# Prompt attention: small and large query blocks in turn

## The chip, the cores and the metric

The kernel runs on one core of one Trainium2 chip. The metric is the device time of one execution in microseconds (us), and for several runs their median. The core has five engines that work beside each other, each through its own list of instructions in program order: PE (matrix products and transposes), DVE (vector work), ACT (activations, copies), POOL and SP (here mostly issuers of DMAs). They wait for each other by semaphores.

## The reference

One decoder layer for a prompt of 16 meta tokens and 1024 tokens, and for 8 sequences of 4 new tokens over a paged cache. In order: norm and input projection, a retention group and an attention group (latent attention, 4 heads), output projection, a gated convolutional feed-forward, a last norm. The change concerns the attention of the prompt alone:

```
def block(args):                      # one block of 128 queries, starting at s0
    ql, qp, s0 = args
    qpos = s0 + jnp.arange(ATTN_BLOCK)
    return mla_attend(ql, qp, ((c_kv, k_pe, kpos[None, :] <= qpos[:, None]),))
...
s = (einsum('bqhc,bkc->bhqk', qf, c_kv) + einsum('bqhr,bkr->bhqk', pf, k_pe)) * SOFTMAX_SCALE
p = softmax(where(mask, s, -inf))     # over the keys
out = einsum('bhqk,bkc->bqhc', p, c_kv)
```

The mask is causal: query block j sees the keys of blocks 0 to j. Block 0 is the 16 meta tokens, blocks 1 to 8 hold 128 queries each. So block 0 has 16 keys, block 1 has 144, and block 8 has 1040.

## The kernel before

The program is a row of stages, each a block in which all five engines run their own lists and at whose end they meet: input projection, latents and retention, prompt attention, decode attention, output projection, feed-forward. Prompt attention works on 36 items (j, h), one for each query block j and head h, in the order of the list `items`: all heads of block 0, then of block 1, up to block 8. Item number i uses half i % 2 of the score banks, of the probabilities `pr` and of the turned probabilities `pt`; the bank of the output is a single one.

For one item:

- PE makes the scores, `score_part` (three products for each piece of up to 512 keys, L1228 to L1230). It waits until the exponentials of item i-2 have left the half (`exped`).
- DVE adds the causal mask on the last 128 columns (L1179), takes the row maximum (L1182) and turns it into the bias (L1190). This is `max_part`. For block 8 the meta keys have scores of their own in `meta_s`, with a maximum (L1182), a joining step (L1188) and later a sum (L1198) more.
- ACT takes the exponential and its row sum (L1145), `exp_part`.
- DVE inverts the sum (L1200) and scales the row (L1203), `scale_part`.
- PE turns the scaled rows, block by block of keys (L1261), `turn_part`, in groups of four blocks. Groups are numbered through all items; group n goes to turn bank n % 2 and waits until group n-2 was copied out. ACT copies the even groups (L1132), DVE the odd ones (L1134), `copy_turn`. An item of block 0 to 3 has one group, of block 4 to 7 two, of block 8 three (four blocks, four, one).
- PE multiplies with the values (L1272), `value_part`, when all groups are copied and the output bank is free (`lo_out` of item i-1).
- ACT takes the output out as a high part (L1152), DVE takes the low part by subtraction (L1208).

What sets the order is the loop of each engine, written out by hand:

```
PE:   score_part(i + 1);  value_part(i - 1);  turn_part(i)
DVE:  scale_part(i);  max_part(i + 1);  odd copies of item i;  lo_part(i - 1)
ACT:  exp_part(i + 1);  even copies of item i;  hi_part(i - 1)
```

SP and POOL meanwhile load six pages of the cache for the stage behind. They wait only for the page table.

Of the kernel before, what the change touches and what calls it, by code (L numbers as in the profile page):

```python
# [37 lines left out]
NT = 1 + SEQ // P  # L38
H, DK = 4, 128
# [16 lines left out]
def col0(j):  # L56
    return 0 if j == 0 else T0 + P * (j - 1)
# [991 lines left out]
def prompt_attention(kit, t, ident, kn, vt, qn, qp, kp, mh, ml, qn_s, qp_s, pages):  # L1049

    nc = kit.nc
    items = [(j, h) for j in range(NT) for h in range(H)]
    with ExitStack() as c:
        causal = kit.sb(c, "pa_causal", [P, P])
        meta_s = kit.sb(c, "pa_meta", [P, H, META])
# [8 lines left out]
        S = {n: kit.sem("pa_" + n) for n in (  # L1064
            "causal", "zero", "meta", "meta_out", "scored", "masked", "max_a", "max_b", "max_c", "exped", "sum_a", "sum_b", "scaled",
            "turned", "act_out", "dve_out", "out_done", "hi_out", "lo_out")}

        def geometry(i):

            j, h = items[i]  # L1070
            return (NS, META, 1) if j == 0 else (col0(j), P, j + 1)

        turns = []
        for i in range(len(items)):
            nb = geometry(i)[2]
            turns += [(i, b, min(b + 4, nb)) for b in range(0, nb, 4)]
# [7 lines left out]
        def scores(i):  # L1084


            j, nq = items[i][0], geometry(i)[1]
            two = score_b[0:nq, 2 * (i % 2):2 * (i % 2) + 2, :].rearrange("p b n -> p (b n)")
            if j < NT - 1:
                return [(two[:, 0:META + P * j], NS, META + P * j)]  # L1090
            return [(two[:, 0:P * j], T0, P * j), (meta_s[0:nq, items[i][1], :], NS, META)]

        with nc.Block() as block:
            @block.sync
            def _(sp):
                sp.dma_start(causal[:], t["causal"]).then_inc(S["causal"], 16)
                pages.load_table(sp)
                sp.wait_ge(pages.table, 16)
                for page in range(EARLY):
                    pages.load_sync(sp, 0, page)  # L1100
                for u in range(EARLY // UP2):
                    pages.wait_unit(sp, 0, u)
# [12 lines left out]
            def copy_turn(n, eng):  # L1115
                i, b0, b1 = turns[n]
                nq = geometry(i)[1]
                eng.wait_ge(S["turned"], n + 1)
                if i >= 2:
                    eng.wait_ge(S["out_done"], i - 1)  # L1120
                runs = []
                if b0 == 0:
                    runs.append((0, 1, T0))
                    b0 = 1
                if b1 > b0:
                    runs.append((b0, b1, P))
                for x0, x1, nk in runs:
                    off = (x0 % 4) * P
                    src = turn_b[0:nk, n % 2, off:off + (x1 - x0) * P].rearrange("p (b q) -> p b q", q=P)[:, :, 0:nq]
                    dst = pt[0:nk, i % 2, x0:x1, 0:nq]  # L1130
                    if n % 2 == 0:
                        m = nc.scalar.activation(dst, src, ACT.Copy)  # L1132
                    else:
                        m = nc.vector.tensor_copy(dst, src)  # L1134
                m.then_inc(S["act_out"] if n % 2 == 0 else S["dve_out"], 1)
# [29 lines left out]
            @block.vector  # L1165
            def _(dve):
                dve.wait_ge(S["causal"], 16)
                dve.wait_ge(S["meta"], H)
                dve.tensor_copy(meta_s[:], extra_b[:, 0, 0:H * META].rearrange("p (h m) -> p h m", h=H)
                                ).then_inc(S["meta_out"], 1)  # L1170
                dve.wait_ge(S["meta_out"], 1)

                def max_part(i):
                    j, nq = items[i][0], geometry(i)[1]
                    dve.wait_ge(S["scored"], i + 1)
                    parts = scores(i)
                    w = META if j == 0 else P
                    own = parts[0][0][:, parts[0][2] - w:]
                    dve.tensor_tensor(own, own, causal[0:nq, 0:w], ALU.add).then_inc(S["masked"], 1)  # L1179
                    dve.wait_ge(S["masked"], i + 1)  # L1180
                    for n, (region, _, _) in enumerate(parts):
                        m = dve.reduce_max(mx[0:nq, i, n:n + 1], region, AX_X)  # L1182
                    m.then_inc(S["max_a"], 1)
                    dve.wait_ge(S["max_a"], i + 1)
                    most = mx[0:nq, i, 0:1]
                    if len(parts) == 2:
                        most = mx[0:nq, i, 2:3]
                        dve.tensor_tensor(most, mx[0:nq, i, 0:1], mx[0:nq, i, 1:2], ALU.max).then_inc(S["max_b"], 1)  # L1188
                        dve.wait_ge(S["max_b"], i + 1 - H * (NT - 1))
                    dve.tensor_scalar(mx[0:nq, i, 3:4], most, -SCALE, None, ALU.mult).then_inc(S["max_c"], 1)  # L1190

                def scale_part(i):
                    j, nq = items[i][0], geometry(i)[1]
                    dve.wait_ge(S["exped"], i + 1)
                    total = sm[0:nq, i, 0:1]
                    if j == NT - 1:
                        total = sm[0:nq, i, 2:3]
                        dve.tensor_tensor(total, sm[0:nq, i, 0:1], sm[0:nq, i, 1:2], ALU.add).then_inc(S["sum_a"], 1)  # L1198
                        dve.wait_ge(S["sum_a"], i + 1 - H * (NT - 1))
                    dve.reciprocal(sm[0:nq, i, 3:4], total).then_inc(S["sum_b"], 1)  # L1200
                    dve.wait_ge(S["sum_b"], i + 1)
                    p = pr[0:nq, i % 2, NS:T0 + P * j]
                    dve.tensor_scalar(p, p, sm[0:nq, i, 3:4], None, ALU.mult).then_inc(S["scaled"], 1)  # L1203

                def lo_part(i):
                    h, (q0, nq, _) = items[i][1], geometry(i)
                    dve.wait_ge(S["hi_out"], i + 1)
                    dve.tensor_tensor(ml[:, H + h, q0:q0 + nq], out_b[:, 0, 0:nq],  # L1208
                                      mh[:, H + h, q0:q0 + nq].bitcast(F32), ALU.subtract).then_inc(S["lo_out"], 1)
                max_part(0)  # L1210
                for i in range(len(items)):
                    scale_part(i)
                    if i + 1 < len(items):
                        max_part(i + 1)
                    for n in range(first_turn[i], last_turn[i] + 1):
                        if n % 2:
                            copy_turn(n, dve)
                    if i:
                        lo_part(i - 1)
                lo_part(len(items) - 1)  # L1220
# [1714 lines left out]
def layer(nc, x, t, y):  # L2935
# [14 lines left out]
    with ExitStack() as c:  # L2950
# [17 lines left out]
        with ExitStack() as c1:  # L2968
            with ExitStack() as c2:
# [32 lines left out]
                with kit.phase():  # L3002
                    prompt_attention(kit, t, ident, kn, vt, qn, qp, kp, mh, ml, qn_s, qp_s, pages)
# [90 lines left out]
```

## Time and profile before

| | us |
|---|---|
| median of 3 runs (1625.48 to 1630.23) | 1627.07 |
| the profiled execution | 1625.34 |
| its span | 1623.7 |
| prompt attention in it, first work of the stage to the last subtraction | 462.30 to 604.30 |
| PE, DVE, ACT busy in the span | 1486.8, 817.5, 590.7 |

The span is what the trace covers; 1.6 us of the execution lie around it. All times below are us from the start of the span. "PEld" is the loading of weights on PE, which overlaps its products. The granted clock is PE's, as a share of 2.4 GHz; its lower level is 1.2 GHz, 0.50.

### The profile page before, as it was taken

The page shows a single profiled execution, that of the slowest core. Times are in us where ns is not written, and L with a number is a line of the kernel's source. Part 1 is how long each engine was busy: PE and PEld are TensorE (multiplying, and loading weights), DVE is VectorE, ACT ScalarE, POOL GpSimd, SP SyncE. Part 2 cuts the span into 40 slices and gives each one's busy share as a digit, 9 for nine tenths or more (in the row PEclk, how much of TensorE's full clock was granted, in tenths as well). Part 3 has the DMA queues.
Part 4 walks back from the last instruction along what each step waited for, and adds up shares of the span by engine and source line. Part 5 has one row for each costly group of instructions (what it writes and reads, how often), then busy time and mean ns, then how long its engine had stood idle before and what let it go on. Part 6 is the DMA issues. An engine that isn't in the chain of part 4 may idle for free. (4 is left out here: it accounts for less than half of the span.)

```text
span 1623.7 us, 26233 instructions
## 1 busy us (share of the span) xinstructions
PE 1486.8 (92%) x9453; PEld 1271.8 (78%) x9453; DVE 817.5 (50%) x1470; ACT 590.7 (36%) x1267; POOL 422.6 (26%) x543
## 2 busy tenths in 40 slices
PE   5999999897989989877997689999999999999997
PEld 5998888665867866555886679999999999778786
DVE  4422200153446644331156756666666565678877
ACT  5420111122433333222033354444544444534454
POOL 3236620130030005524003444443344342000000
PEclk9999999997979999888998899999999999999999
DMA  6422123514230005535132122333332333864764
GB/s 228 145 95 85 61 100 108 177 60 124 84 106 1 1 8 165 156 100 144 58 118 78 48 75 87 104 103 103 103 90 83 98 103 124 302 188 155 247 216 165
DMA packets 142989, 186.76 MB, mean 115 GB/s; under 512 B 22835, under 2 KB 89252, under 8 KB 142710
## 3 DMA queue, kind: packets, MB, share of 16 engines
q1 hardware_dynamic: 137038, 174.37, 33.2%
q0 software_dynamic: 4800, 9.84, 2.1%
q10 hardware_dynamic: 1056, 1.31, 0.3%
q8 instruction: 56, 0.92, 0.2%
q14 instruction: 39, 0.32, 0.1%
HBM read 149.25 MB, written 36.19 MB: 114 GB/s over the span
## 5 line engine op out<-in xcount | busy, mean ns | idle before, releaser
L2779 PE MATMUL p_ff<-s_xh,s_ff_rhi 128*128 128x266 f32 x608 | 178.9, 294 | 33.7 <-ACT s_ff_u L2354 16.8
L2779 PE MATMUL p_ff<-s_ff_th,s_ff_rhi 128*128 128x266 f32 x640 | 183.9, 287 | 0.4 <-DVE s_ff_u L2586 0.4
L2782 PE MATMUL p_ff<-s_ff_th,s_ff_rlo 128*128 128x266 f32 x640 | 183.4, 287 | 0.0
L2781 PE MATMUL p_ff<-s_ff_tl,s_ff_rhi 128*128 128x266 f32 x640 | 183.0, 286 | 0.0
L2782 PE MATMUL p_ff<-s_xh,s_ff_rlo 128*128 128x266 f32 x608 | 176.5, 290 | 0.0
L2781 PE MATMUL p_ff<-s_xl,s_ff_rhi 128*128 128x266 f32 x608 | 176.3, 290 | 0.0
L117 PE MATMUL p_ip<-s_ip_hi,s_xh 128*128 128x512 f32 (+2 forms) x432 | 161.0, 373 | 1.4 <-DVE s_xl L214 1.4
L119 PE MATMUL p_ip<-s_ip_hi,s_xl 128*128 128x512 f32 (+2 forms) x432 | 160.6, 372 | 0.0
L118 PE MATMUL p_ip<-s_ip_lo,s_xh 128*128 128x512 f32 (+2 forms) x432 | 160.5, 372 | 0.0
L2779 PEld LDWEIGHTS p_ff<-s_xh,s_ff_rhi 128*128 128x128 f32 x608 | 117.4, 193 | 44.6 <-issue 22.0
L2887 PE MATMUL p_ff<-s_fd_wh,s_fd_ah 128*128 128x512 f32 x308 | 122.7, 398 | 7.4 <-DVE s_fd_wl L2667 3.4
L2779 PEld LDWEIGHTS p_ff<-s_ff_th,s_ff_rhi 128*128 128x128 f32 x640 | 121.3, 190 | 1.9 <-issue 0.8
L2888 PE MATMUL p_ff<-s_fd_wl,s_fd_ah 128*128 128x512 f32 x308 | 121.3, 394 | 0.0
L2889 PE MATMUL p_ff<-s_fd_wh,s_fd_al 128*128 128x512 f32 x308 | 121.2, 394 | 0.0
L2781 PEld LDWEIGHTS p_ff<-s_ff_tl,s_ff_rhi 128*128 128x128 f32 x640 | 120.9, 189 | 0.0
L2782 PEld LDWEIGHTS p_ff<-s_ff_th,s_ff_rlo 128*128 128x128 f32 x640 | 120.8, 189 | 0.0
L2781 PEld LDWEIGHTS p_ff<-s_xl,s_ff_rhi 128*128 128x128 f32 x608 | 117.5, 193 | 0.0
L2782 PEld LDWEIGHTS p_ff<-s_xh,s_ff_rlo 128*128 128x128 f32 x608 | 117.3, 193 | 0.0
L2544 DVE TENSOR_TENSOR s_ff_rlo<-s_ff_scr,s_ff_rhi 128x512 fp32r<-128x512 f32 x60 | 49.2, 820 | 103.7 <-ACT s_ff_rhi L2340 103.6
L117 PEld LDWEIGHTS p_ip<-s_ip_hi,s_xh 128*128 128x128 f32 x432 | 81.9, 189 | 14.2 <-DVE s_xl L214 1.8
L118 PEld LDWEIGHTS p_ip<-s_ip_lo,s_xh 128*128 128x128 f32 x432 | 81.9, 189 | 12.7
L119 PEld LDWEIGHTS p_ip<-s_ip_hi,s_xl 128*128 128x128 f32 x432 | 81.8, 189 | 12.4
(306 smaller groups left out, 3148.2 us busy)
## 6 DMA issues: line engine op xcount, KB each, us to landing
s_ff_raw<-in_w_up SPq DMA_DIRECT2D x44, 512.0 KB, 4.6
s_fd_lanes<-in_w_down SPq DMA_DIRECT2D x77, 256.0 KB, 3.5
s_fd_lanes<-a_rows SPq DMA_DIRECT2D x66, 256.0 KB, 3.3
a_rows<-s_ff_cv SPq DMA_DIRECT2D x22, 512.0 KB, 3.0
s_ff_scr<-in_w_down SPq DMA_DIRECT2D x11, 1024.0 KB, 6.0
s_ip_raw<-in_w_in SPq DMA_DIRECT2D x4, 2048.0 KB, 8.6
s_pages<-in_cache_kv_latent SPq DMA_DIRECT2D x60, 128.0 KB, 2.2
s_pages<-in_cache_kv_latent POOLq DMA_DIRECT2D x52, 128.0 KB, 2.4
```

The lines of the kernel that those rows point to most:

```text
L117: pe.matmul(out, hi_w, hi_x, start=first, stop=False)
L118: pe.matmul(out, hi_w, lo_x, start=False, stop=False)
L119: return pe.matmul(out, lo_w, hi_x, start=False, stop=last)
L2544: dve.tensor_tensor(rlo[:, s, :], split_source(n, p), rhi[:, s, :].bitcast(F32), ALU.subtract).then_inc(S["lo"], 1)
L2779: pe.matmul(out, rhi[:, s, ks_], hi_cols(k), start=first and k == 0, stop=False, skip_group_check=True)
L2781: pe.matmul(out, rhi[:, s, ks_], lo_cols(k), start=False, stop=False, skip_group_check=True)
L2782: mm = pe.matmul(out, rlo[:, s, ks_], hi_cols(k), start=False, stop=last and k == 3, skip_group_check=True)
L2887: pe.matmul(out, ah[:, r, ts], wh[:, r, :], start=first, stop=False, skip_group_check=True)
L2888: pe.matmul(out, ah[:, r, ts], wl[:, r, :], start=False, stop=False, skip_group_check=True)
L2889: return pe.matmul(out, al[:, r, ts], wh[:, r, :], start=False, stop=last, skip_group_check=True)
```

## The change

The list `items` is put in another order. Before, it went through blocks 0 to 8. Now it takes a small and a large block in turn, head by head: (0, 0), (8, 0), (0, 1), (8, 1), ... (0, 3), (8, 3), then blocks 1 and 7 in the same way, 2 and 6, 3 and 5, and at the end the four heads of block 4. The loops of the engines stay as they are. Two waits of DVE on its own counters, which only items of block 8 have, counted from the place of block 8 in the list; they now count the items of block 8 so far.

```
-    items = [(j, h) for j in range(NT) for h in range(H)]
+    items = [(j, h) for small in range(NT // 2) for h in range(H) for j in (small, NT - 1 - small)]
+    items += [(NT // 2, h) for h in range(H)]
...
+        def last_rows(i):
+
+            return sum(j == NT - 1 for j, _ in items[0:i + 1])
...
-                        dve.wait_ge(S["max_b"], i + 1 - H * (NT - 1))
+                        dve.wait_ge(S["max_b"], last_rows(i))
...
-                        dve.wait_ge(S["sum_a"], i + 1 - H * (NT - 1))
+                        dve.wait_ge(S["sum_a"], last_rows(i))
```

The numbers of the lines behind rise by 5. Groups of turned blocks get other numbers, since they are counted through the list; for block 8 the first and third group are now copied by DVE and the second by ACT, for every head.

How this stands on PE. Before, at two items of block 8: the end of the scores of (8, 2), the values of (8, 0) (nine key blocks), the turns of (8, 1), and the start of the scores of (8, 3). `p_pa_score` is the score bank, `p_pa_out` the output bank, `p_pa_turn` the turn banks, `s_pa_p` the probabilities, `s_pa_pt` the turned ones, `s_wide` holds queries, keys and values.

```order
L1228 MATMUL p_pa_score<-s_wide 128x512
L1229 MATMUL p_pa_score<-s_kp,s_qp 128x512
L1230 MATMUL p_pa_score<-s_kp,s_qp 128x512
L1272 MATMUL p_pa_out<-s_pa_pt,s_wide 128x128 x9
L1261 MATMUL p_pa_turn<-s_ident,s_pa_p 48x128
L1261 MATMUL p_pa_turn<-s_ident,s_pa_p 128x128 x8
L1228 MATMUL p_pa_score<-s_wide 128x512
```

Now, at the turns of (8, 0): the scores of (0, 1), the values of (0, 0), the turns of (8, 0), and the start of the scores of (8, 1).

```order
L1233 MATMUL p_pa_score<-s_wide 16x16
L1234 MATMUL p_pa_score<-s_kp,s_qp 16x16
L1235 MATMUL p_pa_score<-s_kp,s_qp 16x16
L1277 MATMUL p_pa_out<-s_pa_pt,s_wide 128x16
L1266 MATMUL p_pa_turn<-s_ident,s_pa_p 48x128
L1266 MATMUL p_pa_turn<-s_ident,s_pa_p 128x128 x8
L1233 MATMUL p_pa_score<-s_wide 128x512
```

What stood ahead of the turns of a block 8, the scores of the next item and nine blocks of values, is now a small item's 16 columns. The next scores of block 8 stand behind the turns of the block 8 before them in both, but before they were those of the item after the next, and now they are those of the next large item, with only one small item between.

The same on DVE. Before: scaling of (8, 1), the mask and the maxima of (8, 2), the copies of the turned blocks of (8, 1), the low part of (8, 0).

```order
L1203 TENSOR_SCALAR s_pa_p<-s_pa_p,s_pa_sm 128x1040
L1179 TENSOR_TENSOR p_pa_score<-p_pa_score,s_pa_causal 128x128
L1182 TENSOR_REDUCE s_pa_mx<-p_pa_score 128x1
L1182 TENSOR_REDUCE s_pa_mx<-s_pa_meta 128x1
L1188 TENSOR_TENSOR s_pa_mx<-s_pa_mx 128x1
L1190 TENSOR_SCALAR s_pa_mx<-s_pa_mx 128x1
L1134 COPY s_pa_pt<-p_pa_turn 48x128
L1134 COPY s_pa_pt<-p_pa_turn 128x384
L1134 COPY s_pa_pt<-p_pa_turn 128x128
L1208 TENSOR_TENSOR s_xl<-p_pa_out,s_xh 128x128
```

Now: scaling of (8, 0), the mask and the maximum of (0, 1), the copies of (8, 0), the low part of (0, 0), inverse and scaling of (0, 1), and the mask of (8, 1).

```order
L1208 TENSOR_SCALAR s_pa_p<-s_pa_p,s_pa_sm 128x1040
L1184 TENSOR_TENSOR p_pa_score<-p_pa_score,s_pa_causal 16x16
L1187 TENSOR_REDUCE s_pa_mx<-p_pa_score 16x1
L1195 TENSOR_SCALAR s_pa_mx<-s_pa_mx 16x1
L1139 COPY s_pa_pt<-p_pa_turn 48x128
L1139 COPY s_pa_pt<-p_pa_turn 128x384
L1139 COPY s_pa_pt<-p_pa_turn 128x128
L1213 TENSOR_TENSOR s_xl<-p_pa_out,s_xh 128x16
L1205 RECIPROCAL s_pa_sm<-s_pa_sm 16x1
L1208 TENSOR_SCALAR s_pa_p<-s_pa_p,s_pa_sm 16x16
L1184 TENSOR_TENSOR p_pa_score<-p_pa_score,s_pa_causal 128x128
```

Between the scaling of one block 8 and the mask of the next stands now a whole small item, with 16 columns in each step.

## Rows read from the trace of the kernel before

**Rows 1.** Windows: start:end, length, busy of each engine (instructions), clock, DMA share, GB/s.

```profile
470.00:475.00 5.00, 4.27 (x22) 3.81 (x22) 3.11 (x20) 1.46 (x10) 3.06 (x6) 0.50 0.68 198
...
545.00:550.00 5.00, 5.00 (x32) 4.08 (x31) 3.08 (x9) 2.35 (x8) 0.00 (x0) 1.00 0.00 0
...
590.00:595.00 5.00, 3.14 (x27) 2.70 (x25) 2.63 (x7) 2.47 (x8) 0.00 (x0) 1.00 0.00 0
595.00:600.00 5.00, 4.62 (x26) 4.50 (x26) 1.63 (x6) 0.00 (x0) 0.00 (x0) 0.66 0.00 0
```

**Rows 2.** Groups on DVE from 462 to 604: busy, mean ns | idle before, releaser.

```profile
L1179 DVE TENSOR_TENSOR p_pa_score<-p_pa_score,s_pa_causal 128x128 f32<-128x128 f32 x32 | 9.4, 294 | 3.4 <-PE p_pa_score L1230 3.4
```

**Rows 3.** Timeline of DVE, the scalings: start, duration, engine, line, instruction.

```profile
468.20 0.24 DVE L1203 TENSOR_SCALAR s_pa_p<-s_pa_p,s_pa_sm 16x16 f32<-16x16 f32 x1
...
472.43 0.22 DVE L1203 TENSOR_SCALAR s_pa_p<-s_pa_p,s_pa_sm 16x16 f32<-16x16 f32 x1
...
481.76 0.34 DVE L1203 TENSOR_SCALAR s_pa_p<-s_pa_p,s_pa_sm 128x144 f32<-128x144 f32 x1
...
492.33 0.36 DVE L1203 TENSOR_SCALAR s_pa_p<-s_pa_p,s_pa_sm 128x272 f32<-128x272 f32 x1
...
533.55 0.56 DVE L1203 TENSOR_SCALAR s_pa_p<-s_pa_p,s_pa_sm 128x656 f32<-128x656 f32 x1
...
550.27 0.63 DVE L1203 TENSOR_SCALAR s_pa_p<-s_pa_p,s_pa_sm 128x784 f32<-128x784 f32 x1
...
569.63 0.70 DVE L1203 TENSOR_SCALAR s_pa_p<-s_pa_p,s_pa_sm 128x912 f32<-128x912 f32 x1
...
595.53 0.76 DVE L1203 TENSOR_SCALAR s_pa_p<-s_pa_p,s_pa_sm 128x1040 f32<-128x1040 f32 x1
```

**Rows 4.** Timeline of all engines at block 8, 583 to 590 us.

```profile
583.28 2.21 PEld L1272 LDWEIGHTS p_pa_out<-s_pa_pt,s_wide 128*128 128x128 f32 x18
...
583.71 0.30 DVE L1179 TENSOR_TENSOR p_pa_score<-p_pa_score,s_pa_causal 128x128 f32<-128x128 f32 x1 [0.81 <-PE p_pa_score L1230]
...
585.41 0.91 PEld L1261 LDWEIGHTS p_pa_turn<-s_ident,s_pa_p 128*48 128x48 f32 x8
...
585.76 1.11 ACT L1145 ACTIVATE s_pa_p<-p_pa_score,s_pa_mx 128x1024 f32<-128x1024 f32 x1 [4.25 <-DVE s_pa_mx L1190]
586.16 0.75 DVE L1134 COPY s_pa_pt<-p_pa_turn 48x128 f32<-48x128 f32 x2 [0.43 <-PE p_pa_turn L1261]
...
586.96 0.14 PEld L1261 LDWEIGHTS p_pa_turn<-s_ident,s_pa_p 128*128 128x128 f32 x1 [0.64 <-DVE s_pa_pt L1134]
...
587.16 0.58 ACT L1132 ACTIVATE s_pa_pt<-p_pa_turn 128x512 f32<-128x512 f32 x1
...
587.64 0.27 ACT L1152 ACTIVATE s_xh<-p_pa_out 128x128 fp32r<-128x128 f32 x1
...
588.53 0.76 DVE L1203 TENSOR_SCALAR s_pa_p<-s_pa_p,s_pa_sm 128x1040 f32<-128x1040 f32 x1
...
589.97 0.30 DVE L1179 TENSOR_TENSOR p_pa_score<-p_pa_score,s_pa_causal 128x128 f32<-128x128 f32 x1 [0.67 <-PE p_pa_score L1230]
```

**Rows 5.** Timeline at block 6 (one mask) and at block 7.

```profile
546.62 0.29 DVE L1179 TENSOR_TENSOR p_pa_score<-p_pa_score,s_pa_causal 128x128 f32<-128x128 f32 x1
...
562.19 0.91 PEld L1261 LDWEIGHTS p_pa_turn<-s_ident,s_pa_p 128*48 128x48 f32 x8
...
563.06 0.30 PEld L1228 LDWEIGHTS p_pa_score<-s_wide 128*128 128x128 f32 x2
...
565.73 0.30 DVE L1179 TENSOR_TENSOR p_pa_score<-p_pa_score,s_pa_causal 128x128 f32<-128x128 f32 x1 [0.42 <-PE p_pa_score L1230]
```

**Rows 6.** Timeline at the first scores of item (0, 1), and at the stage's end.

```profile
466.86 0.24 PE L1228 MATMUL p_pa_score<-s_wide 128*16 128x16 f32 x2
...
595.35 3.06 PEld L1272 LDWEIGHTS p_pa_out<-s_pa_pt,s_wide 128*128 128x128 f32 x18 [1.11 <-ACT s_pa_pt L1132]
...
604.01 0.29 DVE L1208 TENSOR_TENSOR s_xl<-p_pa_out,s_xh 128x128 fp32r<-128x128 f32 x1 [2.74 <-ACT s_xh L1152]
```

## The prediction

> **What bounds the kernel now.** I read the slices of the profile's page first, to find the stage: prompt attention runs from 462 to 604 us, and nothing else runs beside it but page loads that are over before 490. Then I cut the stage into windows of 5 us, looked at what DVE waits for there, and followed the timeline through one turn of the loop at the large blocks. I call (j, h) an item; blocks 0 to 3 are small, 5 to 8 large.
>
> In the windows PE looks full from 545 on (5.00 of 5.00 us), while its weight loads fill 4.08 [rows 1]. The two readings disagree on whether PE is the bound, so I looked at who waits: DVE waits for scores only 3.4 us in the whole stage [rows 2], such as the 0.81 and 0.42 at blocks 8 and 7 [rows 4, 5]. So before, one loop sets the pace nearly everywhere: DVE scales item i, masks and reduces item i+1, ACT exponentiates it, copies turned blocks of item i, takes out the output of item i-1, DVE takes its low part, inverts, scales item i+1. PE has a whole turn of this loop to prepare the next scores. From scaling to scaling this takes 1.41 us at block 0 ((472.43 - 468.20)/3) and 6.48 at block 8 ((595.53 - 569.63)/4) [rows 3].
>
> The Trainium skill (Trainium Kernel Development and Optimization, "Best Practices") says that matmul busy time is a bad metric and weight-load busy time a good one. By the first the stage's large half would be PE work in any order and the change worth nothing there; by the second there are some 0.9 of 5 us to spare. The 3.4 us of DVE's wait side with the second; the first reading is rival C.
>
> **The change part by part.** The same instructions run with the same shapes; only their order moves, on PE, DVE and ACT. SP and POOL issue what they did, and wait for nothing in the list. The two changed waits count the block-8 items passed, and still name the instruction just ahead of them: nothing, as before.
>
> What matters is PE's program order. In one step PE does the scores of item i+1, the values of i-1, the turns of i. With blocks in order, the scores of the next large item stand a large item ahead of its need. In turn with small ones, a large item's scores stand directly behind the turns of the large item before it, and these wait for its scaling. So scaling, turns, scores, maxima, exponentials of one large item become one serial chain, and all that runs beside it is one small item. DVE's masking of the next large item waits for PE; behind it on DVE stand the low part of the large output and the next scaling, ACT waits for the maximum, and PE's small values for the low part.
>
> Pair 0 and 8, from one large scaling to the next, at the full clock:
> - the scaling takes 0.76, the turns start at 0.8 [rows 3];
> - from the start of the turns to the masking of the next large item 4.56 (585.41 to 589.97): eight transposes, the copy of the first four on DVE (586.16), the ninth that waits for it (586.96), the scores right behind [rows 4]. Order and engine of that copy are the same after the change;
> - masking to exponential 2.05 (583.71 to 585.76), exponential to copy 1.40 (to 587.16), the small item's 16-column copy 0.1 (an estimate; the 512-column one takes 0.48), output to scaling 0.89 (587.64 to 588.53) [rows 4].
>
> Sum 9.8. DVE and ACT finish the small item in between (some 3.5 us, less than 0.8 + 4.56), PE the 18 value matmuls (2.21) behind the scores, so these add nothing. Before, the two cost 1.41 + 6.48 = 7.89: +1.9 a pair.
>
> The first pair is different. The first large scores start where the second small ones did, at 466.86 [rows 6], and the granted clock there is 0.50, the level of 1.2 GHz [rows 1]. At half the clock the 2.7 us of matmuls in the scores take 5.4, so masking comes near 472.3, and 2.05 + 1.40 + 0.4 (sum and inverse) later the first large scaling: 476.2, that is 8.0 after 468.20. The stretch of blocks 0 and 8 becomes 8.0 + 3 x 9.8 = 37.4; it was 4.23 + 25.90 = 30.1 [rows 3]. **+7.3.**
>
> Pair 1 and 7: the turns start at 0.77; turns to masking 3.54 (562.19 to 565.73); masking to scaling 3.90 (565.73 to 569.63), in which ACT copied four blocks (0.53) where it now copies a small item's two, and that only every other time (0.15 on average) [rows 3, 5]. Sum 7.83, against ((481.76 - 472.43) + (569.63 - 550.27))/4 = 7.17. Four pairs +2.6, and 0.8 for the first one, which stands behind the ninth transpose of block 8: **+3.4.**
>
> Pair 2 and 6: the turns wait for three blocks of small values (0.25 each: 2.21 for nine [rows 4]), so they start at 0.78. Turns to masking is 3.54 less one transpose (0.11) and less 128 columns of scores, 0.38 (from 589.97 - 586.96 = 3.01 to 565.73 - 563.06 = 2.67 for 112 columns): 3.05. Masking to scaling 3.65 (546.62 to 550.27), with 0.2 for the copy in place of 0.53 [rows 3 to 5]. Sum 7.16, against (10.57 + 16.72)/4 = 6.82 [rows 3]: **+1.4** for four.
>
> Pair 3 and 5, by the same steps: one block less, masking at 1.02 + 2.56 = 3.6, while DVE and ACT alone need about as long for item 3. No wait is left; block 4 stays among its own. **+0.3** for the odd steps, on 41.2 us (492.33 to 533.55) [rows 3].
>
> The end gains. From the last scaling to the end it took 8.5 us (595.53 to 604.01) plus the last subtraction [rows 3, 6]. The last two items are now of 5 blocks, not 9: two value groups shorter by 4 x 0.25, the first no longer partly at the slow clock (3.06 instead of 2.21), four transposes, and the ninth with its wait (0.5): 2.0 + 0.85 + 0.4 + 0.5 = **-3.7.**
>
> The clock. In a 0/8 pair PE works to 7.6 us (scores, values), then has a little for the small item until the next turns at 10.6. Something like it stands at the end of the kernel before: with PE busy 3.14 of 5 us the clock was still granted in full, in the next 5 it was 0.66 on average, that is 3.4 us at 1.2 GHz [rows 1]. A cold stretch on the turns and scores costs between nothing and 3.3 us (0.45 for transposes, 2.85 for scores) a pair. I take 1.4, a little under half of 3.4, for three pairs, and 0.8 for what is left of it in the first 1/7 pair: **+5.0.**
>
> Sum: 7.3 + 3.4 + 1.4 + 0.3 - 3.7 + 5.0 = +13.7. The profiled run took 1625.34, its span 1623.7 with 1.6 around it: 1639.0. The median of the runs is 1.7 above it. I say **1640**.
>
> **The rivals.**
> - B, the clock stays at 1.2 GHz in the turns and scores of every large item, blocks 7 too. For it: PE's work now comes in bursts. Against it: a 1/7 pair gives PE some 6.9 us of work in 7.8 (turns 0.9, scores 2.7, eight blocks of values 2.0, an estimated 1.3 for the small item). Price 3 x 3.3 + 4 x 3.4 instead of 5: 8.7 + 23.5 = +32, 1657. The Trainium skill (TensorE: Matmul & The Clock Gate, "HAM oscillation") tells of a kernel that paid the change of clock at every burst after a wait, a loss of half the throttled time; the one drop in these windows agrees in kind, not in number.
> - C, no change: PE is the bound from 545 on, as its busy row says, and the same work in another order takes the same time, so that waits gained and lost cancel: 1622 to 1631. Against it: the 4.08 of weight loads, and the serial chain, which needs no full engine.
> - D, faster: small items fill the gaps of the large ones. It decides if the next large scores are in PSUM when DVE gets to them. Then DVE's 3.4 us of waiting go [rows 2], and the end's 3.7: -7, 1618. For it: DVE has 1.9 of 5 us idle between 545 and 550 [rows 1]. Against it: PE's program order, in which those scores cannot stand ahead of the large turns. The Trainium skill (Perfetto Trace Analysis, "Optimization Strategy") says that where the most-contended engine changes over time, interleaving the regimes may help. That is just this change; here no trace bears it out yet, since every item passes all three engines in series.
>
> The order of the built program does what the change says, so that is no rival.
>
> **How the numbers follow.** The forecast 0.74, B 0.11, C 0.08, D 0.07. About 0.3% (4.9 us) is what a measurement can tell from no change. Slower is the forecast and B, 0.85; same 0.08; faster 0.07. The forecast's own bounds are +8.7 with no clock loss (less some 3 for the steps) and +8.7 + 9.9 with the full one in the 0/8 pairs: 1631 to 1644, and somewhat beyond if part of B comes with it. The range is 1631 to 1653; it leaves out D, half of C and the upper half of B.
>
> **What would show it.** Right: scaling to scaling of large items near 9.8, 7.8, 7.2 and 6.9; DVE's wait for scores before masking near 15 to 20 us (3.9 in the first pair, 1.8, 0.9 and 0.4 in a later 0/8, 1/7 and 2/6, and the clock's part) instead of 3.4; a granted clock under 1 in the 0/8 pairs; the end 3 to 4 us shorter. Wrong: scores standing ready at the large masking, PE full throughout with DVE waiting as little as before, or pairs 1/7 to 3/5 no longer than before.

## The result and the profile after

The median after is 1642.72 us (1640.95 to 1643.42, 4 runs) against 1627.22 before (1625.48 to 1630.23, 4 runs): a ratio of 1.0092, 95% interval 1.0074 to 1.0109. The change makes the kernel slower, and the forecast of 1640 (1631 to 1653) holds.

The profiled execution after has a span of 1640.5 us. I read the stage alone, from the first scaling to the end of the last low part: 468.20 to 604.30 before [rows 3, 6], 468.91 to 618.59 after, that is 136.1 and 149.7. The change costs 13.6 us there. The spans differ by 16.8; 0.7 of the rest lies ahead of the stage and 2.5 behind it, where the order of the items changes nothing. These parts scatter: over the ten profiles of this study the first scaling starts between 468.15 and 474.13, and from the stage's end to the program's end it is 1017.0 to 1024.2 us. So a single run's total can be several us off for reasons outside the stage, and the experiments are compared by the stage. The stage itself repeats: the stretch from the last scaling of block 1 to the last of block 7 takes 87.87, 87.83 and 87.88 us in the three runs that leave its order alone (before, only08, end_small).

DVE's timeline of after, the scalings and the first large masking (start, duration, engine, line, instruction); the shape tells the block, as in [rows 3]:

```profile
468.91 0.22 DVE L1208 TENSOR_SCALAR s_pa_p<-s_pa_p,s_pa_sm 16x16 f32<-16x16 f32 x1
...
471.94 0.30 DVE L1184 TENSOR_TENSOR p_pa_score<-p_pa_score,s_pa_causal 128x128 f32<-128x128 f32 x1 [2.81 <-PE p_pa_score L1235]
...
475.90 0.76 DVE L1208 TENSOR_SCALAR s_pa_p<-s_pa_p,s_pa_sm 128x1040 f32<-128x1040 f32 x1
...
487.10 0.76 DVE L1208 TENSOR_SCALAR s_pa_p<-s_pa_p,s_pa_sm 128x1040 f32<-128x1040 f32 x1
...
497.83 0.76 DVE L1208 TENSOR_SCALAR s_pa_p<-s_pa_p,s_pa_sm 128x1040 f32<-128x1040 f32 x1
...
509.99 0.76 DVE L1208 TENSOR_SCALAR s_pa_p<-s_pa_p,s_pa_sm 128x1040 f32<-128x1040 f32 x1
...
519.98 0.70 DVE L1208 TENSOR_SCALAR s_pa_p<-s_pa_p,s_pa_sm 128x912 f32<-128x912 f32 x1
...
543.00 0.70 DVE L1208 TENSOR_SCALAR s_pa_p<-s_pa_p,s_pa_sm 128x912 f32<-128x912 f32 x1
...
571.57 0.63 DVE L1208 TENSOR_SCALAR s_pa_p<-s_pa_p,s_pa_sm 128x784 f32<-128x784 f32 x1
...
613.47 0.49 DVE L1208 TENSOR_SCALAR s_pa_p<-s_pa_p,s_pa_sm 128x528 f32<-128x528 f32 x1
```

From one scaling of block 8 to the next it takes 11.20, 10.73 and 12.16 us, where an item of block 0 and one of block 8 together took 7.89 before. The pairs of blocks 1 and 7 take (543.00 - 519.98)/3 = 7.67, after a first one of 9.99; those of 2 and 6 take (571.57 - 543.00)/4 = 7.14. The lengthening falls from pair to pair with the large item's size, as a serial chain through that item would make it; in the 0/8 pairs the clock has a part in it too.

The same DVE group as [rows 2], from 462 us to the stage's end:

```profile
L1184 DVE TENSOR_TENSOR p_pa_score<-p_pa_score,s_pa_causal 128x128 f32<-128x128 f32 x32 | 9.5, 296 | 18.4 <-PE p_pa_score L1235 18.3
```

The 32 maskings take what they took; DVE's idle time ahead of them went from 3.4 to 18.4 us, and 18.3 of it ends with scores from PE. The timeline of all engines in the second 0/8 pair, the answer to [rows 4], shows why:

```profile
487.10 0.76 DVE L1208 TENSOR_SCALAR s_pa_p<-s_pa_p,s_pa_sm 128x1040 f32<-128x1040 f32 x1
...
487.91 1.50 PEld L1266 LDWEIGHTS p_pa_turn<-s_ident,s_pa_p 128*48 128x48 f32 x8 [0.70 <-DVE s_pa_p L1208]
...
489.00 0.75 DVE L1139 COPY s_pa_pt<-p_pa_turn 48x128 f32<-48x128 f32 x2 [0.69 <-PE p_pa_turn L1266]
489.80 0.18 PEld L1266 LDWEIGHTS p_pa_turn<-s_ident,s_pa_p 128*128 128x128 f32 x1 [0.39 <-DVE s_pa_pt L1139]
489.81 0.61 PEld L1233 LDWEIGHTS p_pa_score<-s_wide 128*128 128x128 f32 x2
...
490.07 1.54 PE L1233 MATMUL p_pa_score<-s_wide 128*128 128x512 f32 x2
...
490.82 0.22 DVE L1208 TENSOR_SCALAR s_pa_p<-s_pa_p,s_pa_sm 16x16 f32<-16x16 f32 x1
...
491.69 0.42 PEld L1233 LDWEIGHTS p_pa_score<-s_wide 128*128 128x128 f32 x2
491.92 1.02 PE L1233 MATMUL p_pa_score<-s_wide 128*128 128x512 f32 x2
...
493.01 2.21 PEld L1277 LDWEIGHTS p_pa_out<-s_pa_pt,s_wide 128*128 128x128 f32 x18
...
493.43 0.30 DVE L1184 TENSOR_TENSOR p_pa_score<-p_pa_score,s_pa_causal 128x128 f32<-128x128 f32 x1 [2.39 <-PE p_pa_score L1235]
...
497.64 0.30 PEld L1277 LDWEIGHTS p_pa_out<-s_pa_pt,s_wide 128*128 128x128 f32 x2 [1.93 <-ACT s_pa_pt L1137]
497.83 0.76 DVE L1208 TENSOR_SCALAR s_pa_p<-s_pa_p,s_pa_sm 128x1040 f32<-128x1040 f32 x1
```

Read it downwards as one chain: large scaling (487.10), its turns (487.91), the ninth transpose behind DVE's copy (489.80), right behind it the next large item's scores (489.81). DVE has scaled the small item by 491.04 and then stands idle for 2.39 us until the scores are there (493.43). Before, the same wait was 0.67 to 0.81 [rows 4]. PE then runs dry in its turn: behind the 18 value products (two instructions for each of nine key blocks), and the small item's few, it waits until the large item comes back scaled.

The windows of after, columns as in [rows 1]:

```profile
470.00:475.00 5.00, 2.31 (x10) 1.14 (x9) 1.91 (x5) 1.01 (x2) 2.96 (x6) 0.84 0.66 182
475.00:480.00 5.00, 3.89 (x14) 2.88 (x14) 2.91 (x12) 1.57 (x9) 3.61 (x6) 0.50 0.64 189
485.00:490.00 5.00, 2.54 (x13) 2.00 (x12) 2.42 (x9) 1.98 (x9) 0.04 (x1) 0.77 0.35 102
490.00:495.00 5.00, 5.00 (x25) 3.59 (x25) 2.22 (x7) 0.52 (x2) 0.00 (x0) 0.89 0.00 0
500.00:505.00 5.00, 5.00 (x11) 2.51 (x10) 1.17 (x6) 0.67 (x2) 0.00 (x0) 0.52 0.00 0
510.00:515.00 5.00, 4.13 (x15) 2.52 (x15) 2.88 (x10) 1.14 (x4) 0.00 (x0) 0.66 0.00 0
515.00:520.00 5.00, 3.91 (x29) 3.42 (x29) 1.94 (x6) 1.59 (x5) 0.00 (x0) 1.00 0.00 0
520.00:525.00 5.00, 4.95 (x30) 3.93 (x31) 3.51 (x11) 1.14 (x4) 0.00 (x0) 1.00 0.01 3
```

In the 0/8 pairs the mean granted clock of a window is under 1 from 465 to 505, down to 0.50 and 0.52, and 1.00 only from 505 to 510. The first 1/7 pair has one more low stretch (0.66 from 510 to 515); from 515 to the stage's end it is 1.00. The window at 500 shows again that a full PE row says little: busy 5.00 of 5, with 10 weight loads instead of the 25 and 31 of the other full windows (490 and 520), at half the clock. The page loads beside the stage do not explain the long pairs: the DMA share is at most 0.01 from 490 on, and the longest pair starts at 497.83.

The end, on all engines, the answer to [rows 6]:

```profile
616.58 1.19 PEld L1277 LDWEIGHTS p_pa_out<-s_pa_pt,s_wide 128*128 128x128 f32 x10 [1.41 <-ACT s_pa_pt L1137]
...
618.30 0.29 DVE L1213 TENSOR_TENSOR s_xl<-p_pa_out,s_xh 128x128 fp32r<-128x128 f32 x1 [1.84 <-ACT s_xh L1157]
```

Ten value products in 1.19 us where eighteen took 3.06, partly at the low clock. From the last scaling (613.47) to the end it is 5.12 instead of 8.77.

### The profile page after: what moved, and what is told of

Its sections match the earlier page's. It is cut to its first block and busy times, and to the rows that moved or that the text cites. A ratio compares the mean times of both kernels' runs of the same rounds, so it can differ in the third digit from the quotient of the medians.

```text
span 1640.5 us, 26231 instructions
## 1 busy us (share of the span) xinstructions
PE 1492.0 (91%) x9453; PEld 1271.8 (78%) x9453; DVE 818.0 (50%) x1478; ACT 589.9 (36%) x1259; POOL 420.5 (26%) x543
## 6 DMA issues: line engine op xcount, KB each, us to landing
s_pages<-in_cache_kv_latent SPq DMA_DIRECT2D x60, 128.0 KB, 2.2
s_pages<-in_cache_kv_latent POOLq DMA_DIRECT2D x52, 128.0 KB, 2.5
```

## The experiments

Theory: the time goes into the place of the large scores in PE's program order, behind the turns of the large item before, and into the clock that PE loses while the chain goes round. Rivals: the loss is not in the 0/8 pairs, or any alternation of sizes costs it, or PE's amount of work is the bound. Each run's number below is the stage as defined above, from one profiled execution; the kernel before has 136.1, the changed one 149.7.

| run | order of the items | stage, us |
|---|---|---|
| only08 | 0 and 8 in turn, the rest in order | 148.0 |
| twos | two small, two large in turn | 152.6 |
| fewer_mixed | as changed, large scores cut by a third | 141.1 |
| warm | as changed, one more group of products in block 8 | 144.7 |
| cut_before | as before, large scores cut to one product | 132.2 |
| cut_mixed | as warm, large scores cut to one product | 128.0 |
| end_small | as before, block 0 last | 134.3 |
| end_small_ahead | as end_small, scores two items ahead | 144.3 |

**only08.** One part alone: of the changed order only the 0/8 pairs.

```
-    items = [(j, h) for small in range(NT // 2) for h in range(H) for j in (small, NT - 1 - small)]
-    items += [(NT // 2, h) for h in range(H)]
+    items = [(j, h) for h in range(H) for j in (0, NT - 1)]
+    items += [(j, h) for j in range(1, NT - 1) for h in range(H)]
```

> Only blocks 0 and 8 in turn, then blocks 1 to 7 in the order of the blocks. I measure the stage from the first scaling to the end of the last low part: 136.1 us before, 149.7 with the change. Serial chain (mine): the loss sits in the large scores that stand behind the turns of the large item before, so the 0/8 stretch costs its 11 us again, from (0, 0) to (8, 3) near 41, block 1 to 7 cost what they did before (some 1.5 more at the step from 8 to 1), and the end, now of 8 key blocks in place of 9, gives back 1 to 2: stage near 147. Rival, the mixing loses evenly in all pairs: a quarter of the 17 us lost ahead of the end, stage near 140.

The run took 1643.21. The 0/8 stretch, from the first scaling to the last one of block 8, is 41.3 us (469.40 to 510.69) against 41.1 in the full change, and its three pairs take 11.25, 10.75 and 12.17, so the loss repeats and does not need the pairs behind it. Blocks 1 to 7 take 100.1 instead of 97.2, the difference lies in the first two steps behind block 8, about twice what was expected. So 11 of the 13.6 us come from the four 0/8 pairs; more than half of what the other pairs add (+6.3) is given back at the shorter end (-3.7).

**twos.** Two large items in a row, so that every second large item has its scores ahead.

```
-    items = [(j, h) for small in range(NT // 2) for h in range(H) for j in (small, NT - 1 - small)]
+    items = [(j, h) for small in range(NT // 2) for two in range(0, H, 2) for j in (small, NT - 1 - small) for h in (two, two + 1)]
```

> Small and large by twos: (0,0) (0,1) (8,0) (8,1) (0,2) ... so that half of the large items follow a large one and the scores of every large item stand behind the turns of a small one, and behind the values of a large one. Serial chain: turns of a large item no longer stand directly ahead of large scores, so only the first large item of each two waits; (0, 0) to (8, 3) falls from 41.1 to 34 to 36 (30.1 before), pairs 1/7 stay near 7.6 to 7.8, stage 139 to 143. Rival, mixing of sizes as such costs (clock, or which engine copies): as many items change size as half before, so at best half the loss goes, (0, 0) to (8, 3) still over 36, or no change at all if the clock drops as often: 149.

A miss: 1645.93, the stage longer than after, not shorter. The 0/8 stretch did shrink (37.5 against 41.1), but stays on the rival's side of 36, and a 1/7 pair takes 9.08 on average instead of 8.25 in after, the first pair counted in both. The timeline of all engines where a block-7 item is followed by one of block 1:

```profile
524.58 0.69 DVE L1208 TENSOR_SCALAR s_pa_p<-s_pa_p,s_pa_sm 128x912 f32<-128x912 f32 x1
524.59 2.66 PEld L1277 LDWEIGHTS p_pa_out<-s_pa_pt,s_wide 128*128 128x128 f32 x16 [2.43 <-ACT s_pa_pt L1137]
...
527.12 1.72 PEld L1266 LDWEIGHTS p_pa_turn<-s_ident,s_pa_p 128*48 128x48 f32 x8
...
529.81 0.28 DVE L1213 TENSOR_TENSOR s_xl<-p_pa_out,s_xh 128x128 fp32r<-128x128 f32 x1
...
530.19 0.29 DVE L1208 TENSOR_SCALAR s_pa_p<-s_pa_p,s_pa_sm 128x144 f32<-128x144 f32 x1
```

The values of the first large item (16 products, 2.66 us) are between the second one's scaling and its turns, which start at 527.12 although the scaling was done at 525.27. The small item's step has no exponential long enough to cover them, and it takes 5.6 us (524.58 to 530.19). The clock has a part in it: it is 0.66 on average from 525 to 530, and the turns' loads take 1.72 us where they took 0.91 before [rows 4]. The step from block 7 to block 2, at a clock of 1.00, takes 3.97. I had left these values out of the sum. It is the same mistake as the change itself makes: a step of the loop in which PE has large work and DVE and ACT have small.

**fewer_mixed.** The changed order; for blocks 5 to 8 only the content product of the scores is kept, the first of the three; the other two are the rotary part.

```
-                        m = score(out, h, slice(q0, q0 + nq), slice(k0, k0 + nk))
+                        if items[i][0] > NT // 2:
+                            m = pe.matmul(out, qn[:, h, q0:q0 + nq], kn[:, h, k0:k0 + nk], start=True, stop=True,
+                                          skip_group_check=True)
+                        else:
+                            m = score(out, h, slice(q0, q0 + nq), slice(k0, k0 + nk))
```

> The changed order, with two of the three score products left out for blocks 5 to 8 (their scores lack the rotary part). Scores of block 8 take some 1.1 us in place of 2.85. Serial chain: PE's scores lie on the path, so the 0/8 pairs fall by 1.75 at the full clock and 2 to 3 with its slow part, the first large item by 3, the 1/7 pairs by 0.9 to where DVE and ACT set the pace, 2/6 by 0.4: stage from 149.7 to 133 to 137, DVE's wait for scores from 18.3 to under 6. Rival, the loss is on DVE, ACT or in the copies: stage falls by no more than the 3 to 4 us that PE was waited for before.

1630.80, stage 141.1: 8.6 shorter than after: longer than the theory said, shorter than the rival said. DVE's wait fell from 18.3 to 11.2. The timeline of all engines in a 0/8 pair:

```profile
487.51 3.29 PE L1255 MATMUL p_pa_score<-s_wide 128*128 128x512 f32 x4
...
490.83 0.30 DVE L1184 TENSOR_TENSOR p_pa_score<-p_pa_score,s_pa_causal 128x128 f32<-128x128 f32 x1 [2.39 <-PE p_pa_score L1255]
```

The kept product still takes 3.29 us for both pieces at half the clock, some 0.82 a piece at the full one, out of 1.32 (in after, from the second piece's first weight load at 491.69 to the first one of the values behind it at 493.01). I had cut a third of the scores and priced it as two thirds. The clock was not held either: it is 0.69 from 485 to 490 and 0.72 from 495 to 500. So the run agrees in direction but does not settle the mechanism; cut_before and cut_mixed go further.

**warm.** The changed order with one more group of three products of 512 columns in each block-8 step, written to a bank that nobody reads, behind the step's scores. It adds PE work and takes none away.

```
+                def warm():
+
+                    pe.wait_ge(S["meta_out"], 1)
+                    score(extra_b[:, 0, :], 0, slice(col0(1), col0(1) + P), slice(col0(1), col0(1) + 512))
+
...
+                    if items[i][0] == NT - 1:
+                        warm()
```

> The changed order, and one more group of three products of 512 columns (1.3 us, into a bank that nothing reads) on PE in each 0/8 pair, in the gap before the small values. Serial chain plus clock: the granted clock stays at 1.00 from the second pair on, the 0/8 pairs fall from 11.2, 10.7 and 12.2 to 9.8, stage from 149.7 to near 145. Rival, the clock is the whole loss: they fall to the 7.9 of before, stage near 139. Rival, the clock is no part of it, or the products are too short to hold it: no change, or longer by up to 1.3 a pair.

1632.64, stage 144.7, as expected. Its windows:

```profile
485.00:490.00 5.00, 3.55 (x20) 2.23 (x21) 2.48 (x10) 2.70 (x10) 0.43 (x1) 1.00 0.43 116
490.00:495.00 5.00, 5.00 (x32) 3.75 (x31) 2.50 (x9) 0.37 (x1) 0.00 (x0) 1.00 0.00 0
500.00:505.00 5.00, 5.00 (x32) 3.96 (x31) 2.19 (x7) 0.69 (x1) 0.00 (x0) 1.00 0.00 0
```

The granted clock is 1.00 from 485 on, and the 0/8 pairs take 10.98 (the clock still rising), 9.69 and 9.68, where the sum without the clock was 9.8. With more work on PE the stage is 5.0 us shorter. That separates the two parts of the loss: at least 5.0 is the clock, and at most 8.6 stays, which is the serial chain less the shorter end. The Trainium skill (TensorE: Matmul & The Clock Gate, "HAM oscillation") describes a kernel that loses time at each burst behind a wait. The windows of after agree in kind, with the 5.0 us over the stage that warm gives back.

**cut_before and cut_mixed.** The scores of blocks 5 to 8 cut to the first rotary product, in the order before and, with the extra group, in the order of warm. The edit, the same in both:

```
-                        m = score(out, h, slice(q0, q0 + nq), slice(k0, k0 + nk))
+                        if items[i][0] > NT // 2:
+                            m = pe.matmul(out, qp[:, h, q0:q0 + nq], kp[:, 0, k0:k0 + nk], start=True, stop=True,
+                                          skip_group_check=True)
+                        else:
+                            m = score(out, h, slice(q0, q0 + nq), slice(k0, k0 + nk))
```

> The order of before, with only one product left of the scores of blocks 5 to 8, the first rotary one, a third of what they take or less (the content part and the low rotary part are left out of their scores). Serial chain: in this order PE has a whole large item's time for the scores, so only DVE's 3.4 us of waiting and the PE limit of blocks 7 and 8 go: intervals into 8 fall from 6.5 to 5.4 to 5.8, into 7 from 4.8 to 4.5, blocks 5 and 6 stay, stage from 136.1 to 130 to 133. Rival, PE's work sets the pace in any order: blocks 5 and 6 fall too, and the stage loses most of the 4 x (2.0 + 1.7 + 1.5 + 1.3) us cut, to under 120.

> The changed order with the same cut of the scores of blocks 5 to 8 and with the group of extra products of the earlier run that held the clock. Serial chain: the scores leave the path, DVE waits for them under 3 us, the 0/8 pairs fall from 9.7 to near 8.0, the first large item comes 4.5 after the first small one in place of 7.0, 1/7 from 7.7 to 6.9, 2/6 from 7.1 to 6.7, 3/5 stay: stage from 144.7 to near 131, within 3 us of the order of before with the same cut, so the loss of the change is the scores' place. Rival, some other loss in mixing (copies on another engine, small items that hide less): it stays 6 us or more above.

1621.35 and 1625.52; the stages are 132.2 and 128.0. The DVE group of [rows 2], first of cut_before:

```profile
L1179 DVE TENSOR_TENSOR p_pa_score<-p_pa_score,s_pa_causal 128x128 f32<-128x128 f32 x32 | 9.4, 293 | 0.2 <-PE p_pa_score L1230 0.2
```

and of cut_mixed:

```profile
L1184 DVE TENSOR_TENSOR p_pa_score<-p_pa_score,s_pa_causal 128x128 f32<-128x128 f32 x32 | 9.3, 292 | 0.0
```

The same cut takes 3.9 us off the order before and 16.7 off the mixed order with its clock held (144.7 to 128.0). Of the 16.7, the 0/8 stretch gives 10.4, the 1/7 stretch 4.6, 2/6 1.4 and 3/5 0.3. A later 0/8 pair falls from 9.7 to 7.6, by about all that the cut takes off the scores of block 8 (an estimated 2.2: two pieces of 1.32, less one rotary product of some 0.24 in each); a later 1/7 pair falls by 1.0, a 2/6 pair by 0.4. So the time of the scores of block 8 is paid nearly in full when they stand behind the turns of block 8, that of the smaller ones in part, and most of it is hidden when they stand an item ahead. Without them DVE's wait is 0.2 us in one order and none in the other, and the mixed one is 4.2 us ahead, about the 3.7 of its shorter end: the alternation by itself costs next to nothing, the place of the scores does. The direct test, the mixed order with PE's scores moved ahead of the large turns, was not run.

The stage of cut_mixed is 3 us shorter than expected. Its total still lies 4.2 above cut_before's, from outside the stage: its first scaling comes 4.6 later (474.13 against 469.56), and the program behind the stage takes 1021.8 against 1017.8. In cut_before two of the four intervals into block 8 are 6.2 instead of the 5.4 to 5.8 expected. In those ACT copies the first turned blocks, behind its exponential (577.69, then 579.09); in the 5.49 between them DVE does (583.82). The mixed order has DVE copy them for every block 8, so up to an estimated 1.5 us of its lead may come from that.

**end_small.** The gain alone: the order before with block 0 moved to the end.

```
-    items = [(j, h) for small in range(NT // 2) for h in range(H) for j in (small, NT - 1 - small)]
-    items += [(NT // 2, h) for h in range(H)]
+    items = [(j, h) for j in [*range(1, NT), 0] for h in range(H)]
```

> The blocks in order but block 0 last: 1 to 8, then 0. It keeps every large item among large ones and ends on the shortest items. After the last block 8 its turns and the values of the item before lie open, some 5.5 us, then three short items and a short end, some 12 in all, where the old list spent 4.2 + 2.2 at its start and 8.8 at its end: 2 to 3 us shorter than before, 1624 to 1625 against 1627. If the turns and values of block 8 lie open longer than that, no difference.

1627.39 (12 runs) against 1628.97 (18 runs of the kernel before, taken beside it), ratio 0.9987, 95% interval 0.997 to 1.0004: not told from no change. In the one profile the stage is 134.3, 1.8 shorter than before, but the step from block 8 to block 0 takes 5.78: the large values and turns in it have no large exponential beside them, and the eighteen value loads take 3.55 us instead of 2.21, with the granted clock at 0.73 from 590 to 595.

**end_small_ahead.** The same, and PE's scores two items ahead, to take them off the chain altogether.

```
                 score_part(0)
+                score_part(1)
...
-                    if i + 1 < len(items):
-                        score_part(i + 1)
+                    if i + 2 < len(items):
+                        score_part(i + 2)
+                    turn_part(i)
...
-                    turn_part(i)
```

> The same list, and PE's loop changed to scores of item i+2, turns of item i, values of item i-1. Scores no longer stand behind the values. At blocks 7 and 8 PE's work per item (scores 2.85, turns 1.2, values 2.2) is what is left as the limit, so intervals into 8 fall from 6.4 to 6.2 at most and those into 7 by 0.1 to 0.3; other blocks are paced by DVE and ACT: 0 to 2 us less than the list alone. If the scores of i+2, which must wait for the exponential of i, hold up the turns of i, it is longer by up to 0.5 an item.

A miss: 1636.74 (7 runs) against 1628.97, ratio 1.0057, interval 1.0037 to 1.0078, slower. DVE's wait for scores is gone (0.8 us instead of 3.9 in end_small). Up to block 7 the intervals stay within some 0.5 of what they were, and the first into block 8 falls from 6.27 to 5.51; the other three become 9.40, 6.81 and 10.08, where end_small has 6.23, 6.40 and 7.01. The timeline of all engines in a long one:

```profile
590.71 0.82 PEld L1265 LDWEIGHTS p_pa_turn<-s_ident,s_pa_p 128*48 128x48 f32 x8 [1.57 <-DVE s_pa_p L1207]
...
592.62 1.11 ACT L1149 ACTIVATE s_pa_p<-p_pa_score,s_pa_mx 128x1024 f32<-128x1024 f32 x1 [3.35 <-DVE s_pa_mx L1194]
...
594.01 0.63 ACT L1136 ACTIVATE s_pa_pt<-p_pa_turn 48x128 f32<-48x128 f32 x2
594.69 0.18 PEld L1265 LDWEIGHTS p_pa_turn<-s_ident,s_pa_p 128*128 128x128 f32 x1 [3.17 <-ACT s_pa_pt L1136]
...
594.88 3.92 PEld L1276 LDWEIGHTS p_pa_out<-s_pa_pt,s_wide 128*128 128x128 f32 x18
```

and its window, columns as in [rows 1]:

```profile
595.00:600.00 5.00, 4.32 (x23) 4.01 (x22) 0.55 (x4) 0.56 (x2) 0.00 (x0) 0.62 0.00 0
```

In every second item of block 8 it is ACT that copies the first turned blocks, behind the exponential. The ninth transpose needs their bank and waits 3.17 us; the values, which this order puts behind the turns, wait with it, and then take 3.92 us instead of 2.21 with the clock at 0.62 in that window. In the order before the values stand ahead of the turns, so that copy holds up only the ninth transpose (1.98 us, at 580.70 in the trace of before) and the scores behind it.

No version here that computes the whole layer beats the kernel before by more than its measurement can tell; cut_before and cut_mixed leave products of the scores out.

## Why the prediction was right

All terms are read from the scalings shown; forecast and measured, in us against the order before:

| term | forecast | measured |
|---|---|---|
| 0/8 stretch, serial chain 7.3 and clock 4.2 | +11.5 | 41.08 - 30.13 = +10.95 |
| 1/7 stretch, 3.4 and clock 0.8 | +4.2 | 33.01 - 28.69 = +4.3 |
| 2/6 stretch | +1.4 | 28.57 - 27.29 = +1.3 |
| 3/5 and 4 | +0.3 | 41.90 - 41.22 = +0.7 |
| end | -3.7 | 5.12 - 8.77 = -3.65 |
| sum | +13.7 | +13.6 |

- **The chain in the 0/8 pair.** The sum of 9.8 at the full clock is measured in warm, where the clock is full: 9.69 and 9.68. (Its 0.48 for ACT's 512-column copy is the time to the next start; the row itself reads 0.58 [rows 4]. Only the estimate of 0.1 rests on it.) The whole 0/8 stretch of warm is 37.4 us (469.28 to 506.66), the number that the prediction had without the clock; that the total fits is partly luck, since its first item took 7.03 instead of 8.0 and its first pair, with the clock not yet held, 10.98.
- **The first large item** was the over-sized term. The prediction took all of its scores at half the clock and came to 8.0 after the first small scaling; it was 6.99. Masking came 3.03 after that scaling (471.94) instead of 4.1: the clock rose during the first large scores, and was 0.84 on average from 470 to 475, where before it was 0.50 [rows 1].
- **The clock** was chosen, at 1.4 a pair between 0 and 3.3. The three pairs came out 11.20, 10.73 and 12.16, that is 1.5, 1.0 and 2.5 above warm's 9.7, and the first 1/7 pair 1.3 above warm's 8.68 (506.66 to 515.34): 6.3 in all, of which warm gives back 5.0, since its own first pair is not held yet. So the clock was some 1.3 dearer than the 5.0 that was forecast and the first item 1.0 cheaper; the two errors nearly cancel, and a sum off by only 0.1 is luck to that extent.
- **The 1/7 pairs.** 7.67 against 7.83, and a first one of 9.99 where 7.83 + 0.8 + 0.8 = 9.4 was said. In the stretch the two cancel again.
- **DVE's wait** for scores: 18.3, forecast 15 to 20. In warm, at the full clock, the mask of a later 0/8, 1/7 and 2/6 pair waits 1.96, 0.86 and 0.17 to 0.33, where 1.8, 0.9 and 0.4 were said; the first large one waits 2.81 in after, where 3.9 was said.
- **Rival B** (clock low in blocks 7 too) falls with the 1.00 from 515 on; only the first 1/7 pair had a low stretch. **Rival C** (PE's work bounds in any order) falls with warm, where more PE work gives 5.0 us less, and with cut_before, where the cut of the scores (an estimated 26 us) takes off only 3.9. **Rival D** (small items fill the gaps) falls by its own condition, since the next large scores are not in PSUM when DVE gets to them. The Trainium skill's advice to interleave regimes (Perfetto Trace Analysis, "Optimization Strategy") is not borne out by this trace, in which doing so costs 13.6 us. cut_mixed shows what the change would need: where those scores take next to no time, alternating costs nothing.

The runs' medians differ by 15.5, the stage by 13.6. The remaining 1.9 is not explained; the parts of the program outside the stage scatter by more than that from run to run.

## What to carry to other kernels

In a software pipeline over in-order engines, write down for each step what each engine does in it, with the items that it belongs to (here scores i+1, values i-1, turns i, exponential i+1). Putting unlike items next to each other pairs one engine's large work with another's small, and what was hidden an item ahead becomes a serial chain; before alternating sizes, ask whether the next large item's first result can stand ahead of the current one's last wait. Then price TensorE's clock as well: here the gaps that the chain opens cost at least 5.0 us, in work done at half the clock.

## What the runs showed that was not expected

- More TensorE work made the kernel shorter: three products of 512 columns more in each block-8 step held the granted clock at 1.00 from 485 us to past 605 and took 5.0 us off the stage.
- The clock rises within a single large item's scores: in the pair shown, the content product of a 512-column piece (two instructions in the trace) took 1.54 us at 490.07 and 1.02 at 491.92 (the timeline of after); the granted clock was 0.50 from 490 to 491 and 1.00 from 492 to 493.
- The content product takes some 0.82 (an estimate, half of what it took at the half clock) of the 1.32 us of a 512-column piece of scores, so the two rotary products together are a little over a third, though they are two of the three products.
